# Prompt attention of a decoder step: probability-times-value products in three f32r passes instead of f32, with the turned probabilities copied as high and low parts

## The reference, cut to what matters

```python
s_cmp = einsum('bqgrd,bngd->bgrqn', qg, kv_cmp[:, :, 0]) * scale      # 31 compressed blocks
p_cmp = masked_softmax(s_cmp, m_cmp)
o_cmp = einsum('bgrqn,bngd->bqgrd', p_cmp, kv_cmp[:, :, 1])
s_sel = einsum('bqgrd,bgqkd->bgrqk', qg, sel[..., 0, :]) * scale      # selected 64-token blocks
p_sel = masked_softmax(s_sel, m_sel)
o_sel = einsum('bgrqk,bgqkd->bqgrd', p_sel, sel[..., 1, :])
s_win = einsum('bqgrd,bkgd->bgrqk', qg, win_kv[:, :, 0]) * scale      # window of 512
p_win = masked_softmax(s_win, m_win)
o_win = einsum('bgrqk,bkgd->bqgrd', p_win, win_kv[:, :, 1])
o = g[..., 0, :] * o_cmp + g[..., 1, :] * o_sel + g[..., 2, :] * o_win
```

## Time and profile before

| | value |
|---|---|
| median of 3 runs | 1969.06 us (1968.24 to 1971.31) |
| profiled execution: its time | 1973.96 us |
| profiled execution: its span | 1972.2 us, granted TensorE clock 0.954 on the mean |
| PE busy | 1779.4 us (90% of the span), 12264 matmuls |
| DVE / ACT / POOL busy | 757.1 (38%) / 666.0 (34%) / 457.8 (23%) us |
| chain that ended last, by engine | PE 80%, DVE 10%, ACT 3%, issue 3% |
| chain, by line | L329 41%, L310 11%, L1287 4%, L490 4% |
| window of the prompt attention (meeting points 4 to 5) | about 1250 to 1496 us of the span |

### The profile page before, as it was taken

How to read it: one execution, slowest core, us unless ns; L and a number is a source line. 1 busy time by engine, 2 the same in 40 slices (tenths; PEclk the granted TensorE clock), 3 DMA queues, 4 the chain that set the end, 5 groups by cost and what they waited for, 6 DMA issues and landing times.

```text
span 1972.2 us, 30496 instructions
## 1 busy us (share of the span) xinstructions
PE 1779.4 (90%) x12264; PEld 1525.8 (77%) x12264; DVE 757.1 (38%) x1435; ACT 666.0 (34%) x1237; POOL 457.8 (23%) x517
## 2 busy tenths in 40 slices
PE   2999897779899999998999899877788899999997
PEld 2555797449899999998999655544447899999996
DVE  2233413513732223226212388445443733223225
ACT  2223323222532123214223456345453443123222
POOL 0000013524610011225113110233232731001124
PEclk9999998689999999999999899689899999999998
DMA  8231231701223222322322755200002223322321
GB/s 264 92 152 43 72 111 43 246 32 65 85 86 86 85 86 85 86 85 72 113 69 68 203 200 193 54 11 12 11 1 64 65 86 86 87 84 85 90 81 46
DMA packets 147969, 176.91 MB, mean 90 GB/s; under 512 B 6220, under 2 KB 139480, under 8 KB 144888
## 3 DMA queue, kind: packets, MB, share of 16 engines
q1 hardware_dynamic: 138568, 113.24, 19.6%
q0 software_dynamic: 9296, 62.21, 8.9%
HBM read 166.61 MB, written 15.05 MB: 92 GB/s over the span
## 4 chain that ended last, share of the span: by engine, by line
PE 80%; DVE 10%; ACT 3%; issue 3%; SPq 2%; POOL 1%; DMA 1%; DVEq 0%; ACTq 0%; POOLq 0%; PEldq 0%
PE ps L329 41%; PE ps L310 11%; PE ps L1287 4%; PE ps L490 4%; PE ps L970 3%; PE ps L974 3%; PE ps L1250 2%; DVE resid L607 2%; PE ps L1270 2%; PE ps L2396 1%; PE ps L2348 1%; DVE arena L954 1%; SPq L889 1%; DVE rstd L456 1%; DVE x_lo L612 1%
## 5 line engine op out<-in xcount | busy, mean ns | idle before, releaser
L329 PE MATMUL ps<-x_hi,w_hi 128*128 128x272 f32 x1248 | 361.3, 290 | 12.2 <-DVEq L245 6.7
L329 PE MATMUL ps<-x_hi,w_lo 128*128 128x272 f32 x1248 | 360.2, 289 | 0.0
L329 PE MATMUL ps<-x_lo,w_hi 128*128 128x272 f32 x1248 | 359.7, 288 | 0.0
L295 DVE TENSOR_TENSOR w_lo<-w_raw,w_hi 128x2048 fp32r<-128x2048 f32 (+1 forms) x94 | 217.0, 2309 | 208.2 <-ACT w_hi L290 208.0
L329 PE MATMUL ps<-h_lo,w_hi 128*128 128x272 f32 x896 | 258.1, 288 | 0.0
L329 PE MATMUL ps<-h_hi,w_hi 128*128 128x272 f32 x896 | 257.9, 288 | 0.0
L329 PE MATMUL ps<-h_hi,w_lo 128*128 128x272 f32 x896 | 257.3, 287 | 0.0
L329 PEld LDWEIGHTS ps<-x_hi,w_hi 128*128 128x128 f32 x1248 | 236.5, 190 | 14.0 <-DVEq L245 7.4
L329 PEld LDWEIGHTS ps<-x_lo,w_hi 128*128 128x128 f32 x1248 | 236.7, 190 | 0.0
L329 PEld LDWEIGHTS ps<-x_hi,w_lo 128*128 128x128 f32 x1248 | 236.6, 190 | 0.0
L290 ACT ACTIVATE w_hi<-w_raw 128x2048 fp32r<-128x2048 f32 (+1 forms) x94 | 177.7, 1891 | 162.2 <-PE ps L329 159.2
(11 more groups left out here) (399 smaller groups left out, 3343.0 us busy)
## 6 DMA issues: line engine op xcount, KB each, us to landing
w_raw<-in_w_up SPq DMA_DIRECT2D x32, 1024.0 KB, 5.4
w_raw<-in_w_down SPq DMA_DIRECT2D x32, 1024.0 KB, 5.6
out_win_s<-in_cache_win_kv SPq DMA_DIRECT2D x8, 1016.0 KB, 14.9
w_raw<-in_w_in_a SPq DMA_DIRECT2D x7, 1024.0 KB, 5.3
w_raw<-in_w_kv_shared SPq DMA_DIRECT2D x6, 1024.0 KB, 5.2
arena<-in_cache_win_kv POOLq DMA_DIRECT2D x5, 1024.0 KB, 10.0
w_raw<-in_w_mem_kv SPq DMA_DIRECT2D x4, 1024.0 KB, 6.0
w_raw<-in_w_out_a SPq DMA_DIRECT2D x4, 1024.0 KB, 5.1
```

The costliest lines, as they stand in the source:

```text
L295: nc.vector.tensor_tensor(w_lo[:, par, 0:n], w_raw[:, par, 0:n], w_hi[:, par, 0:n].bitcast(F32), ALU.subtract).then_inc(split_ready, 1)
L329: mm = nc.tensor.matmul(ps[:, bank + half, 0:HALF], lhsT, rhs, start=k == 0 and x == 0, stop=k == nk - 1 and x == 2)
```

## The change

The value products of the group items (not those of the memory items, nor the compressed ones) run as three f32r passes: high values by high probabilities, low values by high probabilities, high values by low probabilities. For this:

- each turned probability tile of a group item is now copied by both engines: ACT writes the high part, then DVE, which waits for that copy, subtracts it from the same PSUM bank and writes the low part;
- high and low part have 1536 columns each, so there are two places (`pt_pair`) instead of three;
- the values are split once during the memory items: ACT copies four tiles of 512 columns to `vb_hi`, which lies in `w_raw[1]`, in iterations 9 to 12; DVE subtracts them in place of `v_bank` (`vb_lo` has its address) in iterations 10 to 13;
- a value product takes the values of both heads of a pair (128 features) and writes all 128 partitions; only the half of its own head is read;
- because `w_raw[1]` is in use, SyncE loads slot W_OUTB + 1 after the last sum instead of before the attention.

```diff
@@ -200,6 +200,9 @@
                  sb("slc_r2", [P, 4096], F32R, at=addr["xalt"] + 4 * 4096)]
         win_r = [sb("win_r0", [P, 2048], F32R, at=addr["lnbuf"] + 4 * 0), sb("win_r1", [P, 2048], F32R, at=addr["arena"] + 4 * 0), sb("win_r2", [P, 2048], F32R, at=addr["arena"] + 4 * 2048)]
         pt_r = sb("pt_r", [P, 12 * 112], F32R, at=addr["lnbuf"] + 4 * 2048)
+        pt_pair = [sb("pt_pair0", [P, 3072], F32R, at=addr["walt"]), sb("pt_pair1", [P, 3072], F32R, at=addr["walt"] + 4 * 3072)]
+        vb_hi = sb("vb_hi", [P, NQT, 2, 256], F32R, at=addr["w_raw"] + 4 * SLOT)
+        vb_lo = sb("vb_lo", [P, NQT, 2, 256], F32R, at=addr["arena"] + 4 * 6400)
         kcs = sb("kcs", [P, NG, 2, 32], F32R, at=addr["lnbuf"] + 4 * 4096)
         assert base[0] <= nc.sbuf_usable_end, base[0]
...
@@ -1197,31 +1200,38 @@
             return sm[k], sm["past"][k] + n
 
         def att_totals(att):
-            n, events = len(att["items"]), events_before(att, len(att["items"]))
-            owners = [event_reader(att, ev)[0] for ev in range(events)]
-            return {**{k: n for k in ("scored", "max_ready", "exp_done", "weight", "normed")}, "turned": events,
-                    "pt_act": owners.count("act"), "pt_dve": owners.count("dve"), "summed": len(att["jobs"]),
-                    "hi": len(att["outs"]), "lo": len(att["outs"])}
+            n, owners = len(att["items"]), copy_owners(att)
+            return {**{k: n for k in ("scored", "max_ready", "exp_done", "weight", "normed")}, "turned": len(owners),
+                    "pt_act": sum("act" in x for x in owners), "pt_dve": sum("dve" in x for x in owners),
+                    "summed": len(att["jobs"]), "hi": len(att["outs"]), "lo": len(att["outs"])}
 
         def events_before(att, n):
 
             return sum(4 if u["block"] else 1 for u in att["items"][:n])
 
-        def event_reader(att, ev):
+        def copy_owners(att):
 
             owners = []
             for u in att["items"]:
-                owners += ["act", "dve", "act", "dve"] if u["block"] else ["dve" if u["pos"] == u["tiles"] - 1 else "act"]
-            return owners[ev], owners[:ev + 1].count(owners[ev])
+                owners += (["act", "dve", "act", "dve"] if u["block"] else ["act dve"] if u["split"]
+                           else ["dve" if u["pos"] == u["tiles"] - 1 else "act"])
+            return owners
+
+        def copied(att, who, ev):
+
+            return sum(who in x for x in copy_owners(att)[:ev + 1])
 
         def wait_copied(eng, att, sm, ev):
 
-            who, v = event_reader(att, ev)
-            eng.wait_ge(*after(sm, "pt_act" if who == "act" else "pt_dve", v))
+            who = "dve" if "dve" in copy_owners(att)[ev] else "act"
+            eng.wait_ge(*after(sm, "pt_" + who, copied(att, who, ev)))
 
         def pt_place(att, job, parts=P):
 
             j = att["jobs"][job]
+            if j["split"]:
+                place = pt_pair[(j["slot"] + 1) % 2]
+                return [place[:, at:at + j["n"] * j["tiles"]].rearrange("p (c x) -> p c x", x=P * j["tiles"]) for at in (0, 1536)]
             at = 1536 * (j["slot"] % 3)
             return att["pt"][:, at:at + j["n"] * j["tiles"]].rearrange("p (c x) -> p c x", x=P * j["tiles"])
 
@@ -1276,14 +1286,21 @@
                         pe.wait_ge(*after(sm, "lo", j["out"] - 1))
                     if j["block"] is not None:
                         wait_copied(pe, att, sm, j["block"])
-                        mm = nc.tensor.matmul(out, j["v"](0), j["src"], start=True, stop=False)
+                        mm = nc.tensor.matmul(out, j["v"](0), j["src"], start=True, stop=False, skip_group_check=True)
                     else:
                         for t in range(len(items)):
                             if not items[t]["block"] and items[t]["job"] == done:
                                 wait_copied(pe, att, sm, events_before(att, t))
                         pt = pt_place(att, done)
                         chunks = j["n"] // P
-                        for c in range(chunks):
+                        if j["split"]:
+                            pe.wait_ge(v_lo_ready, NQT)
+                            for c in range(chunks):
+                                v_hi, v_lo = j["v"](c)
+                                for v, p in ((v_hi, pt[0]), (v_lo, pt[0]), (v_hi, pt[1])):
+                                    mm = nc.tensor.matmul(ps[:, j["out"] % 2, 0:P * j["tiles"]], v, p[:, c, :], start=False,
+                                                          stop=j["last"] and c == chunks - 1, skip_group_check=True)
+                        for c in range(0 if j["split"] else chunks):
                             mm = nc.tensor.matmul(out, j["v"](c), pt[:, c, :], start=j["first"] and c == 0,
                                                   stop=j["last"] and c == chunks - 1)
                     mm.then_inc(sm["summed"], 1)
@@ -1293,7 +1310,7 @@
 
             u, ev = att["items"][v], events_before(att, v)
             for i in range(NQT if u["block"] else 1):
-                if event_reader(att, ev + i)[0] != who:
+                if who not in copy_owners(att)[ev + i]:
                     continue
                 eng.wait_ge(*after(sm, "turned", ev + i + 1))
                 bank = ps[:, 6 + (ev + i) % 2, :]
@@ -1304,8 +1321,14 @@
                 else:
                     if u["free_at"]:
                         eng.wait_ge(*after(sm, "summed", u["free_at"]))
-                    dst = pt_place(att, u["job"])[:, :, u["pos"] * P:(u["pos"] + 1) * P]
+                    place, at = pt_place(att, u["job"]), slice(u["pos"] * P, (u["pos"] + 1) * P)
                     src = bank[:, 0:u["n"]].rearrange("p (c x) -> p c x", x=P)
+                    if u["split"] and who == "dve":
+                        eng.wait_ge(*after(sm, "pt_act", copied(att, "act", ev)))
+                        nc.vector.tensor_tensor(place[1][:, :, at], src, place[0][:, :, at].bitcast(F32),
+                                                ALU.subtract).then_inc(sm["pt_dve"], 1)
+                        continue
+                    dst = (place[0] if u["split"] else place)[:, :, at]
                 if who == "act":
                     nc.scalar.activation(dst, src, ACT.Copy).then_inc(sm["pt_act"], 1)
                 else:
...
@@ -2137,22 +2161,22 @@
                     n = P * (i + 1)
                     out = NG + NQT * g + i
                     jobs.append({"due": len(items) + 2, "n": 32, "tiles": GQ, "e": e, "out": out, "first": True, "last": False,
-                                 "block": blocks[g]["event"] + i, "src": ptc[:, i, :],
+                                 "split": False, "block": blocks[g]["event"] + i, "src": ptc[:, i, :],
                                  "v": lambda c, g=g: vc_p[:, HD * g:HD * g + HD]})
                     for br in range(2):
                         older = [x for x, j in enumerate(jobs) if j["block"] is None]
                         for r in range(GQ):
                             hd = g * GQ + r
                             q = qs[g % 2][:, r, i * P:(i + 1) * P]
-                            items.append({"block": False, "group": None,
+                            items.append({"block": False, "split": True, "group": None,
                                           "terms": [(q, ks[g % 2][:, br, x, 0:n]) for x in range(2)], "n": n,
                                           "mask": cst[:, C_CAUS + 512 - n:C_CAUS + 512],
                                           "gate": gm[:, i, 3 * hd + 1 + br:3 * hd + 2 + br],
                                           "job": len(jobs), "pos": r, "tiles": GQ,
-                                          "free_at": older[-3] + 1 if len(older) >= 3 else 0})
-                        jobs.append({"due": len(items) - 1, "n": n, "tiles": GQ, "slot": tile_jobs, "e": e, "out": out,
+                                          "free_at": older[-2] + 1})
+                        jobs.append({"due": len(items) - 1, "n": n, "tiles": GQ, "slot": tile_jobs, "split": True, "e": e, "out": out,
                                      "first": False, "last": br == 1, "block": None,
-                                     "v": lambda c, g=g, br=br: v_bank[:, c, br, HD * g:HD * g + HD]})
+                                     "v": lambda c, pr=pr, br=br: [x[:, c, br, P * pr:P * pr + P] for x in (vb_hi, vb_lo)]})
                         tile_jobs += 1
                         if g + 1 < NG and i == NQT - 1 and br == 0:
                             block_item(g + 1)
@@ -2191,6 +2215,9 @@
             return slice(HD * (1 - g % 2), HD * (1 - g % 2) + HD)
 
         def act_prep(act, n):
+            if 9 <= n < 9 + NQT:
+                j = n - 9
+                nc.scalar.activation(vb_hi[:, j, :, :], v_bank[:, j, :, :], ACT.Copy).then_inc(v_hi_ready, 1)
             if n == 0:
                 for e in range(2):
                     half = slice(HD * e, HD * e + HD)
@@ -2207,6 +2234,11 @@
```

(12 more changed lines are left out.)

5 lines of the change are left out of this document (3 added, 2 removed).

## The result

The changed kernel takes **1998.4 us** (median of 4, 1997.2 to 2002.1) where the kernel before takes 1970.2: a ratio of **1.0146** (95% interval 1.0128 to 1.0164), 28.8 us or 1.5% slower. The forecast was 1983.5 us (+14.5) in a range of 1967 to 1997: the side was right, the change twice as large as forecast. The profiled execution took 1997.70 us, with a span of 1996.0.

What follows compares the result with a forecast made beforehand. The prediction took the attention to be bound by a ring through PE and DVE; -10.3 (products) + 9.6 + 14.6 (copies) + 0.6 (values split) = +14.5 us gave a median of 1983.5 us, range 1967 to 1997.

Steps and rivals of the forecast that it cites:

- the ring: Prompt attention: PE and DVE wait for each other, so product savings and DVE work before the third transpose count fully.
- Copies in a cycle without an out: DVE's added subtracts delay the third transpose by 0.6 us (0.3 to 0.8) in each of 16 jobs: +9.6 us.
- a cycle with an out: Every second job: x_hi on ACT delays high copy, subtract and third transpose, +1.15 us in 12; with group ends +14.6 us.
- the group's gap: Four outs close a group, where the next transpose waits 6.05 us anyway: 0.2 us each, 1.15 without that cover.
- Case A: Rival: in the attention the copies hide and only the products count, 1958.8 us (1956 to 1963); chance 0.10.
- case B: Rival: a wash, out cycles at the lower bound and others 0.4 us, +3.5 us, 1972.6 us; chance 0.13.
- case D: Rival: value products don't run at one pass each because of 128-row weights; saving gone, 1993.8 us; chance 0.02.
- values split: Iterations 9 to 13: four ACT copies and four DVE subtracts of 512 columns, mostly covered by PE's products: +0.6 us.
- pile up: Out cycles: x_lo and the block item's turns pile up behind, the upper bound of 1.6 us for the transpose delay.
- A chunk is 0.129 us cheaper: Value products: three f32r passes, 0.516 us, replace f32 at 0.645 us a chunk; 80 chunks, -10.3 us (-9.1 to -13.2).
- -12.9: Value products: alternative price, three passes for four, 0.161 us saved a chunk, -12.9 us; not the one used.
- rival C: Rival: PE's clock stays low through a group's next two jobs, 3 us a group, 12 us in all: 1995.5 us; chance 0.14.

Runs made afterwards that it cites:

- x5: Kernel before plus idle products (PE matmuls nobody reads) in the gaps where groups begin and at the first transpose: 1957.4 us, ratio 0.9939.
- x8: x1 plus the idle products of x3 and 2 more before every third transpose (4 in cycles with an out): 1989.8 us, ratio 1.0102 to the kernel before.
- x9: Changed kernel with the idle products of x3 and 2 more before every third transpose (4 in cycles with an out): 1976.8 us, 1.0034 to the kernel before.
- x7: x2 plus the idle products of x3, none ahead of the third transposes: 1949.4 us, ratio 0.9907 to the kernel before.
- x3: Changed kernel plus idle products (unread PE matmuls) in group-start gaps, after block items' scores and between their turns: 1982.5 us, 1.0067 to the kernel before.
- x2: Changed kernel's three f32r passes, but each turned tile copied once; third pass rereads the high part: 1955.7 us, ratio 0.9929 to the kernel before.
- x1: Changed kernel's copies kept, value products back to one f32 product a chunk from the high parts: 2012.1 us, ratio 1.0220 to the kernel before.
- x10: x9 with x_hi one iteration later on ACT and 2 idle products before every third transpose: 1965.6 us, ratio 1.0004 to the kernel before.
- x6: x3 with x_hi made one iteration later on ACT, behind the next high copy: 1971.5 us, ratio 1.0019 to the kernel before.

## Why the prediction was right in its sign and wrong in its size

**Right: the ring.** Copies in a cycle without an out were put at +0.6 us: cycles 1, 3, 5 and 7 show 0.64, 0.69, about 0.5 and 0.91. In a cycle with an out +1.15: cycles 2 and 4 show 1.33, and 1.06 and 1.03 in group 1 (4.96 - 3.90, 6.17 - 5.14), a mean of 1.19; with x_hi as the named cause, which the move of x_hi confirms. At the group's gap 0.2 us: 0.03 measured in groups 1 and 2. Group 3's last cycle has no gap behind it (5.47 us in x5, for 10.7 and 11.0), and there the copies cost 1.04 (5.84 - 4.80), as the forecast said of a cycle without that cover. Case A, that the copies hide behind idle engines, is refuted by x8 (+32 us), the prediction's case B (a wash, +3.5 us) by x9, and its case D (more than one pass's time for a product) by x7.

All four groups in the forecast's terms, at the high clock (x7's low cycles 5 put at 8.08, x9's at 8.54, and x9's two cycles with idle products in the way at x3's 5.28 and 4.52):

| term | forecast, us | measured, us |
|---|---|---|
| products (x7 less x5), with the last job | -10.3 | -14.5 |
| copies (x9 less x7), 16 cycles without an out | +9.6 | +10.8 |
| copies, cycles with an out and ends of groups | +14.6 | +16.7 |
| values split (memory items, x9 less x5) | +0.6 | +0.3, at clocks of 0.91 and 0.85 |
| sum (of the unrounded terms) | +14.5 | +13.4 |

**Mis-sized: the block item's cycle.** The forecast gave cycle 6 the same 1.15 us; it shows 1.96 (1.68 in group 1: 9.81 - 8.13). There the block item's turns wait for the subtract too (7.0 us for L1273 above), the "pile up" that stood in the bound only. The last group has no block item, and its cycle 6 costs 0.81 (x3's 5.28 less x7's 4.47).

**Mis-sized: the products.** "A chunk is 0.129 us cheaper" is about right for each further chunk: the saving grows from 0.38 us in cycle 1 to 0.55 in cycle 3 (one chunk more) and 0.71 in cycle 7 (two more), 0.11 us a chunk. But a job of a single chunk already saves 0.38 and 0.28 us (cycles 1 and 2). This is x5's and then x7's start of a 128-key product and the scores behind it:

```profile
1350.85 0.86 PE L1298 MATMUL ps<-walt,arena 128*64 128x384 f32 x2
...
1351.64 0.62 PE L1258 MATMUL ps<-ks,qs 128*128 128x384 f32 x2
...
1352.29 0.57 DVE L1403 CUSTOM_DVE_ANT_0 ps<-ps,cst 128x384 f32<-128x384 f32 x1 [1.22 <-PE ps L1258]
```

```profile
1348.66 0.41 PE L1316 MATMUL ps<-pt_pair,vb_hi 128*128 128x384 f32 x1
...
1349.26 0.51 PE L1268 MATMUL ps<-ks,qs 128*128 128x384 f32 x2
...
1349.81 0.57 DVE L1430 CUSTOM_DVE_ANT_0 ps<-ps,cst 128x384 f32<-128x384 f32 x1 [0.82 <-PE ps L1268]
```

From product to scores 0.79 and 0.60 us, from scores to DVE's maximum another 0.65 and 0.55: an f32 job costs a fixed part besides its chunks, before and after the scores. Where a further chunk was priced by the difference of two product chains, that part had dropped out. With it group 2 saves 3.89 us (the sum of x5's row less that of x7) and the four groups 14.0 (3.5, 3.9, 3.4 and 3.3), 14.5 with the last job; by the ratios the products are worth 14 us from before to x2, 13.4 from x8 to x9, and 6.3 from x5 to x7, each within about 6. The forecast's own -12.9 by the Trainium skill ("FP8 and Floating Point Precision", TensorE Precision Notes; four passes to three) lies nearer than its -10.3, though the fixed part shows that it is not four passes against three alone.

These errors cancel: the products give back 4.2 us more than forecast and the copies cost 3.3 more. That the ring's sum of +14.5 came out within about 1 us of the measured +13.4 is luck on top of a right mechanism. (The prediction also read the earlier trace rows a little wrong: ACT is busy 24.84 us there, not 25.7, and PE 41.86, not 41.5. No term rests on it.)

**The step that failed: the clock was left out of the sum.** It stood only as rival C, "the low level may last through the next two jobs" of a group, for 12 us at a chance of 0.14, argued from shorter products and longer waits. The sum took the durations of before as they stood, at 0.50 where before was at 0.50 and at 1.00 elsewhere, and put what the new waits do to the clock at nothing. The runs show 14 to 16 us for it, which is the whole miss: 28.8 less the 14.4 of the ring by the ratios, 29.0 less 13.4 by the profiles. C's price is near that, but from other places. Against the high-clock times of the same cycles, after loses 5.1 us in the first two cycles of the groups, where C put it, and before loses 5.0 there already. In cycles 5 to 8, behind the block item's scores and turns, after loses 13.4 us and before 1.7; the memory items take 2.8 us more, and cycles 3 and 4 1.3. Of C's two reasons the waits are the main one, as x1 shows (52 of the 61 us of low time), and the short products a small one (10 in x2).

## What to carry to other kernels

Before adding waits to a ring through PE, look at the granted clock of the stage that holds it. At 0.88 the stage was already losing 12 us to the low level, and what the change added was paid once in the ring (some 14 us) and once more in the clock (some 15); when costing such a change, give the clock its own term, sized by what low time costs in the traces at hand. The same look shows a gain that neither kernel had: 80 idle products in waits that nobody fills make the kernel before 0.6% faster (x5), and the best placement of x_hi plus idle products brings the change itself from +1.5% to the time of before (x10, 1.0004). Neither makes the change pay: x5 stays ahead of x10 by 0.65%. Idle products belong where a wait is sure: the last two places of x9 had none, and cost 1.3 us. To price a kind of matmul, take the whole job from product to product, not the difference of two chains of products.

## What the runs showed of the hardware

- An f32r pass of 384 columns with 128x128 weights costs 0.32 us start to start at the low clock (1348.29 to 1348.61 in the changed kernel, below), and in x10 0.18 at the high one (1359.75 to 1359.93, from its `vb_lo` record to the next).

```profile
1348.29 0.52 PE L1301 MATMUL ps<-pt_pair,vb_lo 128*128 128x384 f32 x1
1348.61 0.84 PE L1301 MATMUL ps<-pt_pair,vb_hi 128*128 128x384 f32 x2
```

- In the changed kernel the clock was at 0.50 through 8.00 busy us of 8.00 (1342 to 1350 above; PE's ends are modelled), in a stretch of transposes, scores and products that follows waits of 0.88 and 1.36 us.
- One and the same kernel took 1962 us with a mean clock of 0.970 and 1979 with 0.958 (x6).

What stays open: why the low level is left late in one place and early in another, so that cycle 5 of x9 takes 8.54 us in one group and 10.02 and 10.04 in the next two; what exactly in the waits brings it down; and the split of the values with its four copies and subtracts, which was not tried alone (the memory part of x9 is 0.3 us longer than x5's, 51.1 us for 50.9, but at a clock of 0.91 for 0.85, so this bounds little).
